# A hybrid trunk's mixture of experts: the rows of all rounds but the last go through a DRAM buffer instead of a scatter product in each round

## The reference, cut to what matters

```
logits = h @ router_w                       # 256 x 8
top_vals, top_idx = top_k(logits, 2)
top_w = softmax(top_vals)                   # two gates for each token
for e in range(8):
    y += gates[:, e] * (silu(h @ wg[e]) * (h @ wu[e])) @ wd[e]    # 1024 -> 2816 -> 1024
x = x + y
out = rms_norm(x, final_norm)
```

## Time and profile before

| | |
|---|---|
| median of three runs | 1502.67 us (1502.21 to 1503.87) |
| time of the profiled execution | 1501.82 us |
| its span | 1500.1 us |
| TensorE matmul busy | 1461.4 us (97%) |
| VectorE busy | 1216.0 us (81%) |
| ScalarE busy | 883.7 us (59%) |
| GpSimd busy | 75.4 us (5%) |
| DMA | 390.01 MB, mean 260 GB/s over the span |

### The profile page before, as it was taken

The page is one execution under the profiler, slowest core; times in us unless marked ns, Lnnn a source line. Parts: engine busy times, 40 slices in busy tenths (PEclk is TensorE's granted clock), DMA queues, the critical chain, the costliest instruction groups (busy, mean ns, idle before and its releaser), DMA issues.

```text
span 1500.1 us, 23286 instructions
## 1 busy us (share of the span) xinstructions
PE 1461.4 (97%) x8809; PEld 1233.3 (82%) x8809; DVE 1216.0 (81%) x1298; ACT 883.7 (59%) x883; POOL 75.4 (5%) x123
## 2 busy tenths in 40 slices
PE   7999999999999999998999999999999999999997
PEld 5788888999998888787788888888888888888885
DVE  7898786576456787867998989889898898898986
ACT  5234653434334346644677767776767777676774
POOL 2900100000000000101000000000000000000000
PEclk9899999999999999999999999999999999999999
DMA  6444444554364442452999999999999999998993
GB/s 248 154 130 165 153 154 183 197 183 169 94 225 189 162 169 73 167 211 100 367 361 364 359 346 360 361 354 361 345 355 372 343 358 357 349 372 341 356 357 137
DMA packets 76504, 390.01 MB, mean 260 GB/s; under 512 B 28177, under 2 KB 28305, under 8 KB 29970
## 3 DMA queue, kind: packets, MB, share of 16 engines
q1 hardware_dynamic: 74816, 387.61, 68.9%
q10 hardware_dynamic: 1618, 1.44, 0.3%
HBM read 385.21 MB, written 1.05 MB: 257 GB/s over the span
## 4 chain that ended last, share of the span: by engine, by line
PE 87%; DVE 7%; ACT 2%; issue 1%; SPq 1%; DMA 1%; POOL 1%; DVEq 0%; ACTq 0%; POOLq 0%
PE psum L1785 26%; PE psum L1787 26%; PE psum L1786 26%; PE psum L1801 3%; DVE w_lo L579 2%; PE psum L2099 1%; SPq L674 1%; ACT w_hi L573 1%; PE psum L1852 1%; PE psum L1897 1%; PE psum L1834 1%; ACT square_out L834 0%; PE psum L2128 0%; PE psum L2132 0%; PE psum L1827 0%
## 5 line engine op out<-in xcount | busy, mean ns | idle before, releaser
L579 DVE TENSOR_TENSOR w_lo<-w_raw,w_hi 128x2048 fp32r<-128x2048 f32 x267 | 607.2, 2291 | 141.8 <-ACT w_hi L573 140.7
L573 ACT ACTIVATE w_hi<-w_raw 128x2048 fp32r<-128x2048 f32 x267 | 508.1, 1914 | 244.7 <-PE psum L1787 216.4
L1785 PE MATMUL psum<-w_hi,hsT_hi 128*128 128x512 f32 x448 | 176.0, 393 | 1.0 <-DVE hsT_lo L1670 1.0
L1787 PE MATMUL psum<-w_lo,hsT_hi 128*128 128x512 f32 x448 | 174.5, 390 | 0.0
L1786 PE MATMUL psum<-w_hi,hsT_lo 128*128 128x512 f32 x448 | 174.3, 389 | 0.0
L1785 PE MATMUL psum<-w_hi,hT_hi 128*128 128x512 f32 x384 | 156.6, 408 | 4.9 <-DVE w_lo L579 4.8
L1787 PE MATMUL psum<-w_lo,hT_hi 128*128 128x512 f32 x384 | 152.0, 396 | 0.0
L1786 PE MATMUL psum<-w_hi,hT_lo 128*128 128x512 f32 x384 | 151.4, 394 | 0.0
L579 DVE TENSOR_TENSOR w_lo_more<-w_raw,w_hi_more 128x2048 fp32r<-128x2048 f32 x56 | 128.1, 2287 | 9.8 <-ACT w_hi_more L573 8.8
L1785 PE MATMUL psum<-hT_hi,w_hi 128*128 128x256 f32 x416 | 117.6, 283 | 4.1 <-DVE act_ff L1529 2.1
L1787 PE MATMUL psum<-hT_lo,w_hi 128*128 128x256 f32 x416 | 117.2, 282 | 0.0
(11 more groups left out here) (401 smaller groups left out, 2776.5 us busy)
## 6 DMA issues: line engine op xcount, KB each, us to landing
w_raw<-in_stream SPq DMA_DIRECT2D x323, 1024.0 KB, 5.6
w_raw_more<-in_stream SPq DMA_DIRECT2D x40, 1024.0 KB, 6.7
gain_row<-in_gain_rows SPq DMA_DIRECT2D x3, 512.0 KB
x_tok<-in_x SPq DMA_DIRECT2D x1, 1024.0 KB, 5.1
uT_lags<-uT_by_lag SPq DMA_DIRECT2D x64, 16.0 KB, 1.9
zT_by_lag<-uT_lags SPq DMA_DIRECT2D x64, 16.0 KB, 1.8
s_direct<-s_direct_lags SPq DMA_DIRECT2D x40, 16.0 KB, 2.0
s_b_raw<-in_s_b SPq DMA_DIRECT2D x2, 256.0 KB, 8.8
```

The costliest lines, as they stand in the source:

```text
L573: nc.scalar.activation(split_of(seg, i)[0], raw_of(seg, i), ACT.Copy).then_inc(s_hi, 1)
L579: nc.vector.tensor_tensor(l_, raw_of(seg, i), h.bitcast(F32), ALU.subtract).then_inc(s_lo, 1)
L1785: mm(out, lh, rh, start=start, stop=False)
L1787: return mm(out, lh, rl, start=False, stop=stop)
```

## The change

For rounds 0 to 6 the output rows (128 x 1024) are copied out of PSUM by ScalarE as plain float32 into `y_slots`, and ScalarE's queue issues one transfer of 512 KB to the DRAM buffer `y_rows[r]`. VectorE writes no low part, TensorE does no scatter and no choice-matrix transposes, and VectorE does no additions in these rounds. VectorE's three memsets of `selectT`, `y_slots_hi` and `y_slots_lo` ahead of round 0 go.

GpSimd works out, once the routing is there, which row of `y_rows` holds each token's first and second choice, and whether it is in the last round (36 small instructions). In the last round VectorE casts these numbers to integers ahead of slot 5; GpSimd then issues four indirect transfers (128 rows of 4 KB each: two halves of the tokens by two choices) into `x_normed`, the last two when VectorE has added the first two, and VectorE adds each times a gate, two ahead of slot 10 and two ahead of slot 20. The choice matrix is transposed ahead of slot 32 of the last round, and only the last round's own rows go through the scatter.

In the second mixer stage ScalarE's queue issues two transfers that copy `x` into the rows of `y_rows` from row block 7 on, so that rows of rounds that don't take place hold finite numbers.

```
-ROUND_TR = ["ST0", "ST1"] + [f"act{j}" for j in range(NB)]
+ROUND_TR = [f"act{j}" for j in range(NB)]
+LAST_TR = ROUND_TR + ["ST0", "ST1"]
...
+        y_rows = nc.dram_tensor("y_rows", (MAX_ROUNDS, P, D), F32, kind="Internal").ap()
... GpSimd, after the constants
+            pool.wait_ge(s_route, 1)
+            own.do(G_.tensor_scalar(beyond[:, :, :], placed[:, :, :], float(P), None, ALU.is_gt))
+            own.do(G_.tensor_tensor(later[:, :], overc[:, :], iota8[:, :], ALU.subtract))
+            own.settle()
...
+            G_.memset(rowd[:, :], 0.0).then_inc(s_idx, 1)
+            pool.wait_ge(s_idx, 2)
+            for c in range(2):
+                for q in range(NT):
+                    if c:
+                        pool.wait_ge(s_gadd, q + 1)
+                    G_.indirect_dma_start(xn[:, q, :], None, y_rows.rearrange("r p d -> (r p) d"),
+                                          bass.IndirectOffsetOnAxis(ap=rowi[:, c, q:q + 1], axis=0)).then_inc(s_g[q], 16)
... ScalarE, second mixer stage
+                    if l == 1 and s in (10, 14):
+                        n = EXPERTS - 1 + (s - 10) // 2
+                        act.dma_start(y_rows[n:n + 2, :, :], t["x"].rearrange("(t p) d -> t p d", p=P)).then_inc(s_yz, 16)
... ScalarE, a round's end
-                    nc.scalar.activation(ysh[:, c * 512:(c + 1) * 512], bank(c), ACT.Copy).then_inc(s_ysh, 1)
+                    if c == 0 and not first:
+                        act.wait_ge(s_yw, r * 16)
+                    nc.scalar.activation((ysh if last else yrow)[:, c * 512:(c + 1) * 512], bank(c), ACT.Copy).then_inc(s_ysh, 1)
+                if not last:
+                    act.wait_ge(s_ysh, r * 2 + 4)
+                    act.dma_start(y_rows[bass.ds(r, 1), :, :].rearrange("o p d -> (o p) d"), yrow[:, :]).then_inc(s_yw, 16)
... VectorE
-            own.do(V.memset(ST[:, :].bitcast(F32), 0.0))
-            V.memset(ysh[:, :].bitcast(F32), 0.0).then_inc(s_ysh, 2)
-            V.memset(ysl[:, :].bitcast(F32), 0.0).then_inc(s_ysl, 2)
+            V.memset(gcol[:, :], 0.0).then_inc(s_ysh, 2)
+            def add_rows(c):
+                for q in range(NT):
+                    dve.wait_ge(s_g[q], 16 * (c + 1))
+                    if c:
+                        dve.wait_ge(s_gadd, q + 1)
+                    V.scalar_tensor_tensor(x[:, q, :], xn[:, q, :], wgt[:, c, q:q + 1], x[:, q, :], ALU.mult, ALU.add).then_inc(s_gadd, 1)
...
-                    if i == 3:
-                        scattered(r)
+                    if last and i == 5:
+                        dve.wait_ge(s_idx, 1)
+                        dve.wait_ge(s_yw, r * 16)
+                        V.tensor_copy(rowi[:, :, :], rowf[:, :, :]).then_inc(s_idx, 1)
+                    if last and i in (10, 20):
+                        add_rows(i // 10 - 1)
+                    if last and i == SEG - 1:
                         for q in range(NT):
...
-                for c in range(2):
+                for c in range(2 if last else 0):
                     dve.wait_ge(s_ysh, r * 2 + (2 + c + 1))
... TensorE
-                            pe.wait_ge(s_scatv, r * 4 + 2)
+                            pe.wait_ge(s_act, r * NB + GU0)
...
-                        pe.wait_ge(s_scatv, r * 4 + 4)
+                        pe.wait_ge(s_ysh, r * 2 + 2)
...
-                    if i == 3:
-                        scatter(r)
+                    if last and i == SEG - 1:
                         for q in range(NT):
```

More of the change, by code:

```diff
@@ L459, in trunk @@
         s_y0 = sem("y_first_half_written")
+        s_yw, s_gadd, s_idx = sem("y_rows_stored"), sem("rows_added"), sem("row_numbers_ready")
+        s_g = [sem(f"rows_fetched_{q}") for q in range(NT)]
+        s_yz = sem("further_rows_filled")
         s_xh, s_xl = sem("x_normed_hi_ready"), sem("x_normed_pieces_ready")
@@ new lines, in _ @@
+            own.settle()
+            own.do(G_.tensor_tensor(at_row[:, :, :], at_row[:, :, :], beyond[:, :, :], ALU.add))
+            for c in range(2):
+                own.do(G_.tensor_tensor(mine[:, c, 0], over_q(iota8[:, :]), topf[:, :, c:c + 1].to_broadcast([P, NT, 8]), ALU.subtract))
+            own.settle()
+            for c in range(2):
+                own.do(G_.tensor_scalar(mine[:, c, 0], mine[:, c, 0], 0.0, None, ALU.is_equal))
+            own.settle()
+            for c in range(2):
+                own.do(G_.tensor_tensor(mine[:, c, 1], mine[:, c, 0], at_row[:, :, :], ALU.mult))
@@ new lines, in _ @@
+            own.settle()
+            for c in range(2):
+                own.do(G_.tensor_tensor(mine[:, c, 0], mine[:, c, 0], at_round[:, :, :], ALU.mult))
+            own.settle()
+            for n in (4, 2, 1):
+                for c in range(2):
+                    own.do(G_.tensor_tensor(mine[:, c, :, :, 0:n], mine[:, c, :, :, 0:n], mine[:, c, :, :, n:2 * n], ALU.add))
+                own.settle()
+            for c, g_ in enumerate((g1, g2)):
+                own.do(G_.tensor_scalar(in_last[:, c, :], mine[:, c, 0, :, 0], rF[:, 1:2], None, ALU.is_equal))
+                own.do(G_.tensor_tensor(rowd[:, :] if c == 0 else rowf[:, 1, :], mine[:, 1 - c, 1, :, 0], mine[:, c, 1, :, 0], ALU.subtract))
@@ L1037, in _ @@
                 hs_hi(bank(2 + g), g)
+            act.wait_ge(s_yz, 32)
             act.wait_ge(s_route, 1)
@@ L1766, in _ @@
             own.settle()
-            scattered(rounds, last=True)
+            scattered()
             dve.wait_ge(s_gf, 16)
@@ L2115, in _, with scatter @@
             last_round = pe.value_load(rI[0:1, 1:2], min_val=EXPERTS - 1, max_val=MAX_ROUNDS - 1)
-            def scatter(r, last=False):
+            def scatter():
+                pe.wait_ge(*freed(TR0 + LAST_TR.index("ST1"), last_round))
+                pe.wait_ge(*freed(TR0 + LAST_TR.index("ST0"), last_round))
                 for c in range(2):
@@ L2129, in scatter @@
                     if c == 0:
[L2130 removed]
+                        pe.wait_ge(s_ysl, 1)
                     for tk, b in two:
@@ L2207, in _ @@
             pe_round(last_round, last=True)
-            scatter(rounds, last=True)
+            scatter()
 def by_chunk(a, n):
```

56 lines of the change are left out of this document (42 added, 14 removed).

## The result

The changed kernel takes 1488.82 us (median of five runs, 1485.91 to 1489.63), the kernel before 1502.67 us beside it (five runs, 1501.70 to 1503.88). The ratio is 0.9905, with a 95% interval of 0.9892 to 0.9919: faster by 13.9 us, where 17.2 were forecast, and 3.3 us above the forecast of 1485.5, inside the range. The profiled execution took 1489.63 us, its span is 1487.8.

The account below looks back on a forecast made before the run. TensorE was taken to set the pace in the rounds, with loads and splits ahead of it. 18.4 - 0.5 - 0.5 - 0.2 = 17.2 us saved, median 1502.67 to 1485.5 us, range 1482.5 to 1492.5 us.

Parts of the forecast that it names:

- The scatter in each round: TensorE's scatter products and choice-matrix transposes: removing them saves 2.00 us in each of eight rounds, 16.0 us.
- Round 0: 4.4 us won, 1.0 lost: Round 0: scatter and slot 4 stop go (TensorE 4.4 us earlier); 0.5 lost to VectorE's thin margin, 0.5 to GpSimd.
- The row stores: Seven stores of 0.52 MB on ScalarE's queue: 0 us, as 369 GB/s is under what the trace had borne.
- The rival that took 356 GB/s for the ceiling: Rounds: DMA becomes the bound, 1.3 us more in each of 7 rounds, 1508 us, slower; chance 0.05.
- VectorE's additions in round 7: Last round: four additions, 2.5 us per pair ahead of slots 10 and 20, less than the 3.2 us borne before; 0 us.
- The four indirect transfers: Last round's fetch of rows: each 512 KB should land in 2 to 6 us, in time for VectorE; 0 us.
- the fetch is late: Last round: with transfer time T, TensorE stops 2T - 18 us, then about 2T - 30; 1518 us at T = 20; chance 0.06.
- The prediction's own sign of being wrong: New profile: TensorE gaps behind `w_lo` in many rounds, or one long gap in round 7, would show the prediction wrong.
- The fills: Second mixer stage: two 1 MiB copies of `x` into `y_rows`, 5.6 us each if spread over all engines; 0 us, at most 4.
- The estimate of 20 us: Mixer fills: outermost dimension 2 means two DMA engines, 20 us each; in the partly-given-back rival, 1489 to 1494 us, chance 0.16.
- The choice matrix at slot 32: Last round: its transposes move to slot 32, so 0.18 us on TensorE comes back; counted as 0.2 us lost.
- at most 1 us: Round 0 in the new profile: no 2.27 us stop at slot 4, later TensorE stops at most 1 us.

Follow-up runs that it names:

- the kernel with the split first: The changed kernel with fetches issued one at a time, and VectorE splitting slot 1 ahead of the first gathered rows' low parts; 1488.49 us, ratio 0.9906.
- that with GpSimd later: The changed kernel with GpSimd's 36 row-number instructions started only behind VectorE's extra work in round 0 (behind slot 21); 1488.50 us in one run.
- the spread version: The changed kernel with the four fetches issued at slots 5, 10, 15, 20 and added at 12, 17, 22, 27; 1486.69 us, ratio 0.9896.

## Why the prediction was right, and where it was off

*The scatter in each round, 2.00 us.* Measured 97.27 - 95.25 = 2.02 us in each of six rounds. Right, and the order "TensorE sets the pace, loads and splits follow" held: between 808 and 1370 us ScalarE waited 29.6 us in 23 waits for `w_raw` (22.1 for `w_hi`, 7.5 for `w_hi_more`), three times the 9.1 us of the earlier trace rows, and TensorE never stopped.

*Round 0: 4.4 us won, 1.0 lost.* Measured 88.69 - 85.23 = 3.46 against 3.4. The size is right in this execution, and that is luck: it has the shortest stop of all ten, and in the others of the change and its variants (the kernel with the split first left out) round 0 took 85.54 to 88.43 us, 0.3 to 3.2 less than before. Half of the reason is not right. GpSimd's instructions were stretched, from some 0.2 us to as much as 2.4 us, and took from 709.36 to 737.93 us, but VectorE's splits beside them stayed at 2.28 to 2.31 us, so neither the 1.4 us that the prediction gave for it on VectorE nor its estimate of 10 us came out, and without GpSimd the stop was no shorter. The loss is late loads, as the ten profiles show, named in the prediction as the condition of its 0.5 us ("only if ScalarE and the loads follow"), and it differs between executions: the stop was 0.61 us here, 2.14 us in the second profile of the same kernel and 1.1 to 2.4 in the others. In two of these (stops of 2.14 and 2.38 us) TensorE then ran 3.4 us at half its clock, another 1.7 us: the second profile of the change kept only 0.6 us in round 0 (88.12 us).

*The row stores, 0 us.* Right at one store of 0.52 MB in a round; with four, a round takes 1 to 2 us more.

The rival that took 356 GB/s for the ceiling falls: the DMA went at 421 to 425 GB/s with a share of 1.01 to 1.02, loads and stores together. The Trainium skill's page HBM Reference, "Specifications (TRN2)", says that a core that streams alone measures about 425 GB/s, bounded by its 16 DMA engines, and gets some 358 only while its neighbour streams too; the trace agrees with the first figure, and the second, which the prediction quoted, is not for a core alone.

*VectorE's additions in round 7, 0 us.* Right: 1.28 and 1.29 us for the first pair with a wait of 0.97 us for the transfer between them, 2.47 for the second pair; without the fetch they stopped nobody.

*The four indirect transfers, 0 us.* This is the term that was mis-sized: it measured 3.1 us in this execution, 3.0 in the second profile of the same kernel and 1.8 in that with GpSimd later (last part 107.10 us), whose last round is the same. The working took a landing of 2 to 6 us from loads on a free DMA and asked only whether the rows would be there in time for VectorE. They nearly were: VectorE stood 0.97 us for the second of them, of the 4 us that it was given ahead of TensorE. The rival "the fetch is late" counted 2T for a pair; with T = 10.9 that is a stop of 3.8 us. But the two of a pair ran side by side, 15.1 us from the first issue to the second landing, and the stop that the chain has behind them, at 1422.00, cost 0.51 us. The prediction didn't ask what 2.1 MB more do to the loads beside them, in a stretch where the DMA has a share of 0.93 to 1.01 without them. 2.1 MB at 422 GB/s are 5.0 us of a full DMA; 1.8 to 3.1 came out on TensorE. That the lead of the splits swallowed the rest is argued, not shown. The prediction's own sign of being wrong, one long gap in round 7, came true at 1466.71 with 1.87 us, a long way behind the fetched rows.

*The fills, 0 us.* Right: 6.5 us to landing, and no stop behind them. The estimate of 20 us by the rule on the outermost dimension in the Trainium skill's DMA: Bandwidth & Descriptors, "Why a DMA increments its semaphore by 16 and not by 1", did not come true for this DRAM-to-DRAM copy with an outermost dimension of 2: the two landed after 6.0 and 7.1 us.

*The choice matrix at slot 32, 0.2 us.* Not measured by itself; with the scatter that goes, 1.8 us were forecast for the last part, and the kernel without the fetch won 1.87.

*The whole.* 17.2 us forecast, 13.9 measured by the medians of the first comparison. The 3.3 between are near the fetch's 3.1, but that is no proof, for the medians also hold a round 0 that in most executions kept less than in the profiled one. The profiled executions' 12.2 have the 2.1 us ahead of the rounds besides. What the prediction named for the new profile came: rounds of 95.25 us (95.3), TensorE busy in all of rounds 1 to 6, the DMA at 369 GB/s (370), no scatter but the last. The one that didn't always is "at most 1 us" for the later stops in round 0: 0.61 us here, more than that in each other profile of these kernels that has the stop.

## What to carry to other kernels

An added transfer has two prices: whether its data come in time, and what it takes from the transfers beside it. For the second, look at the DMA's share in the very stretch where it falls, not at the mean of the stage: where it is full, the loads beside come later. That is only a warning, since the spread version ran a DMA just as full without a stop; whether it costs time is decided by how far the loads fall behind against the lead of the work that needs them. The same four transfers cost up to 3.1 us in two pairs and 0.4 one at a time.

Where a stop differs in length from one execution to the next, put its length beside the time of each event that could cause it in all profiles there are. One of them keeps step with it, and that can show a cause that no single edit isolates.

Before an engine's idle stretch is filled with work, look at whether it is a wait for another engine or the engine's own issue; only the first can be filled.

## What the runs showed of the hardware

- The DMA of one core topped out at 421 to 426 GB/s over stretches of 10 us and more, with a share of 1.01 to 1.02, with loads alone and with loads, stores and indirect transfers mixed.
- An indirect transfer of 128 rows of 4 KB took 0.9 to 3.0 us on GpSimd and landed 7.2 to 12.0 us after its issue beside a full stream of loads (medians of four 9.9 and 10.9); a plain store of the same 512 KB took 8.2.
- Small GpSimd instructions of 0.2 us took up to 2.4 us beside VectorE's splits, and the splits (two inputs in SBUF, 2.29 us) grew by 0.02 us at most.
- Behind stops of 2.1, 2.4, 3.2 and 7.3 us TensorE ran 3.3 to 3.9 us at 1.2 GHz; behind one of 1.7 us (clock 1.00 from 1466.7 to 1470.0) it did not, and behind one of 2.3 us in the kernel before (1.00 from 725.0 to 728.5) it did not either. In the kernel with seven more stores six stops of 2.4 to 3.6 us had such a spell behind them and four of 2.8 to 3.6 us had none (1.00 from 820 to 824, 840 to 844, 922.4 to 926 and 1455.3 to 1459). So a stop of 2 us may cost 1.7 us more, and its length alone doesn't tell whether it does.
- Of eight stores of 512 KB issued one behind the other the first held the issuing engine for 0.37 us and the other seven for 5.3, 0.75 us each.
- A weight load of 1 MiB that came late in round 0 stopped TensorE for just as long, to 0.04 us, in ten profiles: 0.61 us of stop with its split at 20.97 us, 2.38 with 22.75.
